# The query blocks of the sparse attention in the order 3, 2, 1, 0

## The reference

```
def one_block(args):                      # 4 blocks of 128 queries, one after the other
    qb, iqb, iwb, pb = args
    logits = einsum('bthd,bsd->bths', iqb, ik32) * IDX_DIM ** -0.5       # 8 index heads of 64
    scores = einsum('bths,bth->bts', relu(logits), iwb * IDX_HEADS ** -0.5)
    scores = where(causal, scores, -inf)
    _, idx = top_k(scores, 128)
    k_sel, v_sel = k[idx], v[idx]                                        # one key/value head
    s = einsum('bthd,btkd->bthk', qb, k_sel) * A_HEAD_DIM ** -0.5        # 4 query heads of 128
    p = softmax(where(valid, s, -inf))
    return einsum('bthk,btkd->bthd', p, v_sel)
```

## Time and profile before

| | us |
|---|---|
| median of 3 runs | 1915.96 (1913.83 to 1917.14) |
| the profiled execution | 1925.78 |
| its span, first to last instruction | 1924.0 |
| TensorE busy | 1893.1 |
| VectorE busy | 1133.0 |
| ScalarE busy | 486.9 |
| granted TensorE clock, mean | 0.993 |

### The profile page before, as it was taken

How to read it: one execution, slowest core, us unless ns; L and a number is a source line. 1 busy time by engine, 2 the same in 40 slices (tenths; PEclk the granted TensorE clock), 3 DMA queues, 4 the chain that set the end, 5 groups by cost and what they waited for, 6 DMA issues and landing times.

```text
span 1924.0 us, 24975 instructions
## 1 busy us (share of the span) xinstructions
PE 1893.1 (98%) x8814; PEld 1533.2 (80%) x8814; DVE 1133.0 (59%) x1920; ACT 486.9 (25%) x963; POOL 352.9 (18%) x549
## 2 busy tenths in 40 slices
PE   8999999999999999999999999999999999999998
PEld 6877777788788888888878767777888888888887
DVE  6865788843476542454477657887534755425534
ACT  3163353312334100011222533434032331000101
POOL 2221111111220222222112211111112102222220
PEclk9999999999999999999999999999999989999999
DMA  6432222321521322322223322222215222222221
GB/s 241 141 118 87 66 72 80 93 74 58 205 91 54 110 91 96 99 98 99 77 88 99 122 73 74 77 80 88 70 61 220 66 77 98 98 92 95 97 99 55
DMA packets 73053, 186.78 MB, mean 97 GB/s; under 512 B 18368, under 2 KB 30848, under 8 KB 72064
## 3 DMA queue, kind: packets, MB, share of 16 engines
q1 hardware_dynamic: 41904, 152.10, 23.4%
q10 hardware_dynamic: 31056, 33.38, 5.2%
HBM read 174.40 MB, written 11.06 MB: 96 GB/s over the span
## 4 chain that ended last, share of the span: by engine, by line
PE 94%; ACT 3%; DVE 2%; issue 1%; DMA 0%; DVEq 0%; SPq 0%; ACTq 0%
PE psD L1090 24%; PE psD L1092 24%; PE psD L1091 24%; PE psM L1092 4%; PE psM L1091 4%; PE psM L1090 4%; PE psM L1149 2%; PE psM L1163 1%; PE psM L1358 1%; PE psM L1255 1%; PE psM L1156 1%; PE psM L1376 1%; PE psM L1364 1%; PE psM L1382 1%; PE psM L1247 1%
## 5 line engine op out<-in xcount | busy, mean ns | idle before, releaser
L1090 PE MATMUL psD<-a_hi,w_hi 128*128 128x512 f32 (+2 forms) x1488 | 599.2, 403 | 2.4 <-DVE a_lo L2267 1.5
L1092 PE MATMUL psD<-a_hi,w_lo 128*128 128x512 f32 (+2 forms) x1488 | 579.0, 389 | 0.0
L1091 PE MATMUL psD<-a_lo,w_hi 128*128 128x512 f32 (+2 forms) x1488 | 578.2, 389 | 0.0
L1000 DVE TENSOR_TENSOR w_lo<-raw,w_hi 128x1024 fp32r<-128x1024 f32 x208 | 254.0, 1222 | 294.8 <-POOL w_hi L1068 293.8
L1067 POOL TENSOR_TENSOR w_hi<-raw,tabs 128x1 fp32r<-128x1 f32 x272 | 62.6, 230 | 1532.8 <-PE psD L1092 1323.5
L1090 PEld LDWEIGHTS psD<-a_hi,w_hi 128*128 128x128 f32 (+1 forms) x1488 | 282.6, 190 | 75.1 <-issue 18.5
L1091 PEld LDWEIGHTS psD<-a_lo,w_hi 128*128 128x128 f32 (+1 forms) x1488 | 282.8, 190 | 58.9 <-issue 4.8
L1092 PEld LDWEIGHTS psD<-a_hi,w_lo 128*128 128x128 f32 (+1 forms) x1488 | 282.2, 190 | 58.1
L1068 POOL TENSOR_SCALAR w_hi<-raw 128x1023 fp32r<-128x1023 f32 x272 | 299.2, 1100 | 0.0
L1869 ACT CAST f_hi<-gt 128x512 f32 x64 | 39.9, 623 | 484.8 <-DVE gt L2302 479.6
L2299 DVE TENSOR_SCALAR gt<-psD 128x512 f32<-128x512 f32 x64 | 44.3, 692 | 146.8 <-PE psD L1092 146.8
(11 more groups left out here) (273 smaller groups left out, 2562.8 us busy)
## 6 DMA issues: line engine op xcount, KB each, us to landing
raw<-in_ws SPq DMA_DIRECT2D x272, 512.0 KB, 3.2
s_raw<-in_wo ACTq DMA_DIRECT2D x14, 512.0 KB, 11.6
x<-rows_d ACTq DMA_DIRECT2D x4, 1024.0 KB, 5.8
x<-out ACTq DMA_DIRECT2D x2, 2048.0 KB, 8.2
e_raw<-in_wo ACTq DMA_DIRECT2D x8, 512.0 KB, 6.8
tabs<-in_tab SPq DMA_DIRECT2D x1, 2944.0 KB, 11.2
x<-in_x SPq DMA_DIRECT2D x4, 512.0 KB, 5.2
out<-x SPq DMA_DIRECT2D x4, 512.0 KB, 8.8
```

The source lines that it names most:

```text
L1000: dve.tensor_tensor(w_lo[:, s, :], raw[:, s, :], w_hi[:, s, :].bitcast(F32), ALU.subtract) \
L1090: pe.matmul(out, lhi, rhi, start=start, stop=False)
L1091: pe.matmul(out, lhi, rlo, start=False, stop=False)
L1092: return pe.matmul(out, llo, rhi, start=False, stop=stop)
```

## The change

`BLOCK_ORDER = (3, 2, 1, 0)` gives the order of the query blocks; the loop over blocks in the planner follows it. Where the planner and the kernel took the block before or the number of earlier operations from the block's number, they now take it from the order: `TURN` (the place of a block), `LOGITS`, `SCORES` and `SPREAD` (how many index logits, score steps and transposes come before it). The z slabs wait for the last index pair of block 1, which is now the last with an indexer, and the split of mixer C waits for the attention output of block 0.

```
+BLOCK_ORDER = (3, 2, 1, 0)
+TURN = {tb: i for i, tb in enumerate(BLOCK_ORDER)}
+RANKED = [tb for tb in BLOCK_ORDER if tb]
+LOGITS = {tb: IH * i for i, tb in enumerate(RANKED)}
+SCORES = {tb: (IH + 1) * i for i, tb in enumerate(RANKED)}
+SPREAD = {tb: sum(t + 1 for t in BLOCK_ORDER[:i]) for i, tb in enumerate(BLOCK_ORDER)}
...
-    for tb in range(ST):
+    prev = ranked = None
+    for tb in BLOCK_ORDER:
...
-                q = IH * (tb - 1) + i
-                ring = [("dve", "index", (q - 2) // IH + 1, (q - 2) % IH)] if q >= 2 else [("pe", "rv", H - 1, ST - 1)]
+                q = LOGITS[tb] + i
+                ring = [("dve", "index", RANKED[(q - 2) // IH], (q - 2) % IH)] if q >= 2 else [("pe", "rv", H - 1, ST - 1)]
...
-                   after=[("act", "index", tb, i), ("dve", "index", tb, i - 1) if i else ("dve", "top", tb - 1, TOPS - 1)])
+                   after=[("act", "index", tb, i), ("dve", "index", tb, i - 1) if i else ("dve", "top", ranked, TOPS - 1)])
...
-                   + [("dve", "smax", tb - 1, H - 1)] * (part == TOPS - 1))
+                   + [("dve", "smax", prev, H - 1)] * (part == TOPS - 1))
+            ranked = tb
...
-               after=[("dve", "turn", ROTS - 1), ("pe", "rv", H - 1, ST - 1), ("dve", "top", tb, TOPS - 1), ("pe", "pt", tb - 1, tb - 1), ("act", "pt", tb - 1, tb - 1)])
+               after=[("dve", "turn", ROTS - 1), ("pe", "rv", H - 1, ST - 1), ("dve", "top", tb, TOPS - 1), ("pe", "pt", prev, prev),
+                      ("act", "pt", prev, prev)])
...
-    split("C", [("act", "attend", ST - 1), ("act", "ret", H - 1), ("dve", "fin", "C", H - 1)])
+    split("C", [("act", "attend", BLOCK_ORDER[-1]), ("act", "ret", H - 1), ("dve", "fin", "C", H - 1)])
...
-        slab("z", h, to=[("dve", "z", h)], order=("z", h - 1) if h else None, after=[("pe", "index", ST - 1, IH // 2 - 1)])
-        op("act", "z", h, t=copied(), after=[("pe", "z", h), ("pe", "index", ST - 1, IH // 2 - 1)])
+        slab("z", h, to=[("dve", "z", h)], order=("z", h - 1) if h else None, after=[("pe", "index", RANKED[-1], IH // 2 - 1)])
+        op("act", "z", h, t=copied(), after=[("pe", "z", h), ("pe", "index", RANKED[-1], IH // 2 - 1)])
```

More of the change, by code:

```diff
@@ L329, in schedule @@
             op("act", "prob", tb, h, t=copied(w), after=[("dve", "rinv", tb, h)])
-        f = tb * (tb + 1) // 2
         for m in range(tb + 2):
@@ L333, in schedule @@
                 op("pe", "pt", tb, m, t=.44, to=("act", "pt", tb, m), after=[("act", "prob", tb, h) for h in range(H)])
-                ring = [("pe", "av", tb, m - 2)] if m >= 2 else [("pe", "av", tb - 1, tb - 1)]
+                ring = [("pe", "av", tb, m - 2)] if m >= 2 else [("pe", "av", prev, prev)]
                 op("act", "pt", tb, m, t=copied(), after=[("pe", "pt", tb, m)] + ring)
@@ L338, in schedule @@
         op("act", "attend", tb, t=copied(), after=[("pe", "av", tb, tb)])
+        prev = tb
     def split(br, over):
@@ L952, in drained @@
             if k == "il":
-                return [("relu", IH * (a[0] - 1) + a[1] + 1)]
+                return [("relu", LOGITS[a[0]] + a[1] + 1)]
             if k == "as":
-                return [("smax", H * a[0] + a[1] + 1)]
+                return [("smax", H * TURN[a[0]] + a[1] + 1)]
             if k == "pt":
-                return [("pt", a[0] * (a[0] + 1) // 2 + a[1] + 1)]
+                return [("pt", SPREAD[a[0]] + a[1] + 1)]
             if k == "ao":
-                return [("oa", a[0] + 1)]
+                return [("oa", TURN[a[0]] + 1)]
             if k == "fin":
@@ L972, in mid @@
             elif name[0] == "ao":
-                eng.wait_ge(*on("att_pv", (name[1] + 1) * (name[1] + 2) // 2))
+                eng.wait_ge(*on("att_pv", SPREAD[name[1]] + name[1] + 1))
             else:
@@ L1367, in pt_ @@
                     def pt_(tb, m):
-                        pe.wait_ge(*on("prob", H * (tb + 1)))
+                        pe.wait_ge(*on("prob", H * (TURN[tb] + 1)))
                         turn_heads(("pt", tb, m), lambda h: pr[:, h, cut(m)])
                     def av(tb, m):
-                        i = tb * (tb + 1) // 2 + m
+                        i = SPREAD[tb] + m
                         pe.wait_ge(*on("va_in", 1))
@@ L1710, in index @@
                         ps = mid(act, ("il", tb, i))
-                        q = IH * (tb - 1) + i
-                        if q >= 2:
-                            act.wait_ge(*on("score", 9 * (tb - 1) + i - 1 if i >= 2 else 9 * (tb - 1)))
+                        if LOGITS[tb] + i >= 2:
+                            act.wait_ge(*on("score", SCORES[tb] + i - 1 if i >= 2 else SCORES[tb]))
                         sig(act.activation(rl[:, i % 2, 0:(tb + 1) * P], ps[:, 0:(tb + 1) * P], ACT.Relu,
@@ L1717, in sexp @@
                     def sexp(tb, h):
-                        act.wait_ge(*on("nmax", H * tb + h + 1))
+                        act.wait_ge(*on("nmax", H * TURN[tb] + h + 1))
                         w = slice(0, (tb + 1) * P)
@@ L1724, in prob @@
                         w = slice(0, (tb + 1) * P)
-                        act.wait_ge(*on("rinv", H * tb + h + 1))
+                        act.wait_ge(*on("rinv", H * TURN[tb] + h + 1))
                         sig(act.activation(pr[:, h, w], pr[:, h, w], ACT.Copy, scale=rinv[:, h:h + 1]), "prob")
                     def pt_(tb, m):
-                        i = tb * (tb + 1) // 2 + m
+                        i = SPREAD[tb] + m
                         ps = mid(act, ("pt", tb, m))
@@ L1773, in swish @@
                         if kind == "z" and h == 0:
-                            mid(act, ("il", ST - 1, IH - 1))
+                            mid(act, ("il", RANKED[-1], IH - 1))
                         dst = (gt if kind == "cg" else iq)[:, h, :]
@@ L2126, in index @@
                         w = slice(0, (tb + 1) * P)
-                        q = IH * (tb - 1) + i
-                        dve.wait_ge(*on("relu", q + 1))
+                        dve.wait_ge(*on("relu", LOGITS[tb] + i + 1))
                         ww = iw[:, tb * IH + i:tb * IH + i + 1]
@@ L2159, in smax @@
                             own("picked")
-                            mid(dve, ("pt", tb - 1, tb - 1))
+                        if TURN[tb]:
+                            other = BLOCK_ORDER[TURN[tb] - 1]
+                            mid(dve, ("pt", other, other))
                         ps = mid(dve, ("as", tb, h))
@@ L2168, in recip @@
                     def recip(tb, h):
-                        dve.wait_ge(*on("sexp", H * tb + h + 1))
+                        dve.wait_ge(*on("sexp", H * TURN[tb] + h + 1))
                         sig(dve.reciprocal(rinv[:, h:h + 1], rsum[:, h:h + 1]), "rinv")
```

## The result

| | before | after |
|---|---|---|
| median of the plain runs | 1915.96 (1913.83 to 1917.28, 5 runs) | 1926.18 (1924.50 to 1927.47, 5 runs) |
| the profiled execution, its span | 1925.78, 1924.0 | 1926.18, 1924.4 |
| TensorE busy | 1893.1 | 1884.3 |
| TensorE idle (span less busy) | 30.9 | 40.1 |
| mean granted clock in the plain runs | 0.998 to 0.999 (from later runs of the same kernel that took 1914 to 1917) | 0.993 to 0.994 |

The ratio is 1.0052, with a 95% interval of 1.0040 to 1.0063: the new order is slower by 10.2 us. The forecast was 1911.4, with a range to 1921, so both sign and range were wrong. The stages and the waits are therefore compared, not the spans.

A forecast was written before the change was run, and what follows sets the result against it. TensorE, busy 98%, was taken as the bound, leaving only its idle time or clock to regain. Steps 1 and 2 cost 0; the output 2.3 us earlier per layer gave -4.6 us, 1916 to 1911.4, range 1906 to 1921.

The forecast's parts named there:

- Step 1: Start of the index phase: block 3's index logits replace block 1's; TensorE stays busy 166 of 166 us, cost 0.
- Step 2: Release of the z slabs: last index pair issued at about 319 or 325, slack 15 to 23 us, cost 0.
- Step 3: End of the last top-k on VectorE: at about 366.5 in place of 367.8, bounds 363.5 and 370.
- Step 4: Attention tail, block 1 then block 0: 16.1 us in place of 17.8, plus 0.7 delay; output 2.3 us earlier per layer.
- rival 3: Tail: two short attention chains in series cost latency, +5 to +6 us per layer, 1927; chance 0.12.
- rival 2: Tail: all idle time and the clock dip go, 8.5 us less, 1907.5; chance 0.12.
- Rival 4: z slabs starve if block 1's last index pair comes after 342; 4 us too late is +8, 1924; chance 0.06.

The follow-up runs named there:

- the run with -120: Changed kernel (order 3, 2, 1, 0) with all top-k rounds' ranks lowered by 120 instead of 60 us; 1913.11 us, ratio 0.9981 to the kernel before.

## Why the prediction was wrong

**Step 1 failed, and it decides.** It said of the start that TensorE "has independent slabs to put between; it stays at 166 of 166. Cost 0". The slabs were there, but a slab needs a free PSUM bank as well, and the bank of this one comes free by VectorE. The step that was costed on VectorE, 536 ns more for each of 16 rounds, 8.6 us, was asked only for what it did to the next block, never for what else on VectorE stood behind the block. The earlier trace rows gives the first `index` step of block 1 and the earlier trace rows its last pair of logits; what ran on VectorE right behind its mask, an evacuation done at 244.79, 1.2 us before the dense piece at 245.96, was not read. With so little cover, the 8.6 us of the rounds and the wider passes of the mask became 9.4 us of waiting, and the stretch was busy for 156.10 us of 166. The runs show it from both sides: evacuations ranked higher -17.4 us, half of the rounds -12.5, the old order with longer rounds +30.

**Step 2** holds in its result, not in its numbers. No wait stands at the first `z` slab. The last index pair came at 336.6, and at 331.0 in the version with `cg` ranked higher, where no long wait shifts it; 319 to 325 was forecast. The slack was 5 to 11 us and not 15 to 23, and the run with -120 used it up.

**Step 3** was outside its bounds on the early side: 362.16 + 0.29 = 362.5 where 366.5 (363.5 to 370) was forecast, and 358.3 with `cg` ranked higher:

```profile
362.16 0.29 DVE L2160 TENSOR_SCALAR negb<-negb 128x256 f32<-128x256 f32 x1
```

I let VectorE's idle time change by 2 or 3 us. It changed more: in the 200 to 366 window of that version VectorE is busy for 149.6 us in place of 138.5, so it idles 11 us less. That a wide block at the start is what fills this time is argued, not shown.

**Step 4** has two errors that cancel. ScalarE's last two output copies after:

```profile
377.25 0.59 ACT L1744 COPY qa<-psM 128x512 f32<-128x512 f32 x1
...
383.48 0.59 ACT L1744 COPY qa<-psM 128x512 f32<-128x512 f32 x1 [0.17 <-PE psM L1385]
```

From mask to output it was 384.07 - 362.45 = 21.6 us, where 16.1 + 0.7 was forecast. The forecast cuts this where block 1's last transposed probabilities are copied out and block 0's scores may begin:

```profile
374.19 0.59 ACT L1741 COPY pt<-psM 128x512 f32<-128x512 f32 x1 [0.74 <-PE psM L1172]
...
375.69 0.66 PE L1373 MATMUL psM<-ka,qa 128*128 128x128 f32 x4
```

Block 1's part was 374.78 - 362.45 = 12.3 us, against 10.2 + 0.7. Block 0's was 384.07 - 374.78 = 9.3 against 5.9 (8.4 from the start of its scores), because products of the delta-rule chain and slabs still stand between its steps. So most of the miss, 3.4 of 4.8 us, is in block 0's chain, where rival 3 put it, though short of rival 3's 14 us; from the copy on it is over the 9 us that the prediction named as a sign of being wrong. The output at 384.1 is only 0.8 late against the forecast 383.3, because the mask was early. The first mergeC matmul came at 388.67 (386.6 forecast). And the idle time of the tail did not shrink by 2.3 us but went altogether, as rival 2 had it: slabs, `z` slabs among them, still stand between the steps. That is no gift of the early wait, which pushes slabs back: 23.00 of 23.00 with `cg` ranked higher, at a mask-to-output time of 23.8 us. Latency there costs nothing so long as slabs lie between the steps.

**The rivals.** Rival 3's 1927 is nearly the time that came, for another reason: block 0's chain was longer than forecast, but its price, idle time in the tail, is shown to be absent by the windows. Rival 4 was real, in one of the variants, at the border given. With the `cg` evacuations ranked higher the order gives 1908.8, between my forecast and rival 2's 1907.5; the case that was missing is a long first block whose rounds outrank the evacuations. Its condition (whose rank is higher than whose) could have been read from the planner, and its price from the earlier trace rows and the timeline behind block 1's mask.

## What to carry to other kernels

Before a long chain on one engine is made longer or moved to the front, list what its engine does right behind it, and ask for each item which buffer or bank it frees and who is next in line for it; an engine busy for 83% of a stretch has slack on average and may have none behind that chain. In a list scheduler that ranks by the path behind an operation, a fixed deduction for filler work stops meaning filler as soon as that work moves to the front; here a larger deduction in the old order was worth 15.6 us, and no order of the blocks that was tried came measurably below that. A wait that is removed by hand in a finished order is likely to come back at the next instruction held by the same chain; replan, or move everything that the chain holds.

## What was not expected of the hardware

The profiled execution of the kernel before has a stretch of half clock that most of its runs can't have had, by their times and mean clocks. Slices of 10 us at the start of the MLP, in layer 0 and layer 1:

```profile
610.00:620.00 10.00, 9.28 (x64) 0.83 0.27 72
620.00:630.00 10.00, 10.00 (x37) 0.66 0.82 300
...
1570.00:1580.00 10.00, 10.00 (x52) 0.61 0.75 265
1580.00:1590.00 10.00, 10.00 (x40) 0.88 0.36 124
```

In layer 0, 1.7 + 3.4 = 5.1 us of capacity are lost, in layer 1 3.9 + 1.2 = 5.1, with TensorE busy all the time but for one gap of 0.7 us. The kernel after has the same gap there and a clock of 1.00. These 10.2 us come close to the difference of 9.8 between the execution (1925.78) and the median (1915.96). The same loss stands at the same place, once, in five other profiled executions: with the rounds lowered by 120 (layer 0), with the orders 3, 1, 2, 0 (layer 1) and 2, 3, 1, 0 (layer 0), with the long first block (layer 1), and with the two evacuations moved by hand (layer 0); each time it is 5.1 or 5.2 us. Over 23 plain runs of the kernel before the time goes with the mean clock: 1913.8 to 1914.9 at 0.999, 1915.2 to 1917.4 at 0.998, 1920 to 1922.6 at 0.995 or 0.996, 1925.2 at 0.993. These steps of about 5 us fit none, one or two such stretches, but only the profiled executions show them. What decides it from run to run stays open. A difference of 5 us between two versions is therefore read only after the clock at the start of the MLP has been looked at.
